# Expert results summed on chip: a gate-weighted one-hot product per pair of experts, in PSUM banks open for the layer

## The chip, the cores and the metric

One core of one Trainium2 chip runs the kernel. The metric is device time in microseconds of one execution. Engines: TensorE (PE; its weight loads are PEld), VectorE (DVE), ScalarE (ACT), GpSimd (POOL), SyncE (SP), and 16 DMA engines. PSUM has eight banks of 128 partitions x 512 fp32. All arithmetic is fp32.

## What is computed

One inference step of a two-layer encoder over 288 tokens (256 of a prompt, 32 of a sample), width 1024. Each layer has attention, an output projection, a layer norm, and then a mixture of 16 experts of which each token uses two. What the change touches is this last part:

```
gate = one_hot(the token's two experts) * their normalized scores      # (288, 16)
for e in range(16):
    h = silu(t @ w_gate[e]) * (t @ w_up[e])                            # 1024 -> 512
    y = y + gate[:, e:e + 1] * (h @ w_down[e])                         # 512 -> 1024
x = layernorm(ALPHA * x + y, ln2_g, ln2_b)
```

Between the layers, `x @ w_kv_shared` gives keys and values for layer 1; beside it stands a projection of the memory prompt with `w_mem_kv[1]`, which doesn't need x.

## The kernel before

Everything is written by hand: each engine has its own program, and semaphores order them. The tokens form three tiles (`TOKS`): 128, 128 and 32 rows, in `x_tok`.

**Routing.** VectorE works out for each token its two gates (`gates`) and two row numbers (`row_ab`): expert e has the rows 64e to 64e+63 (`CAP` = 64 slots). Tokens are sorted by expert through DRAM (`sorted_rows`), brought back, turned (`turn_rows`, L959) into `xs`, and each expert's 64 slots are copied to `xg`.

**One expert**, on TensorE, in the order that `expert_order` gives (up 0, up 1, down 0, turn, down 1, up 2, then for e from 3: up e, down e-1; at the end down 15):
- up(e), L916: 16 products, 64 slots stationary, 512 columns of gate and up weights moving, two halves of the array side by side, into bank e%2. ScalarE takes exp (L1378), VectorE forms the hidden values in four steps (L1832 to L1835).
- down(e): two transposes (L923) into bank 2, a copy by VectorE (`hidden_t`, L1825) for which TensorE waits some 0.5 us, then eight products (L930) into bank 3 or 4.
- ScalarE copies the result (L1400) and stores it with two transfers (L1403) to `expert_rows` in DRAM.

**Weights.** SP loads them, three experts ahead: gate and up of e+3 are asked for when up(e) has ended (L528), down of e+3 when down(e) has (L533).

**Combination.** After the stage GpSimd gathers each token's two rows (L2052), and VectorE multiplies them by the gates and adds them to ALPHA x (L1937, L1948). In layer 1 alone (`PAIR = (False, True)`) the last two experts aren't stored: ScalarE copies them into the two halves of `y_pair` (L1411), and TensorE adds them by a one-hot product (`add_tile`, L1026 and L1032) in PSUM, from which VectorE takes the statistics of the norm (L1927, L1932; L1736 finishes it).

**Between the layers** TensorE first turns the memory prompt (`memx1`, L1041) and projects it (`memkv1`, L1049), then turns x tile by tile (L679) and multiplies it by the shared weights (`kvs`, L1176). ScalarE empties memkv1's second bank (L1482, L1483) only after the root for tile 1's norm (L1365), and the same three banks serve kvs. SP asks for the first shared weights after tile 0's gathers.

**More than 64 tokens of one expert** are handled by branches (`more`) that this input doesn't take; both kernels have them.

Of the kernel before, what the change touches and what calls it, by code (L numbers as in the profile page):

```python
# [25 lines left out]
D = 1024  # L26
# [5 lines left out]
P = 128  # L32
# [17 lines left out]
PAIR = (False, True)  # L50
PAIR_ROW = ROWS - 2 * CAP
# [15 lines left out]
for _name, _n in (("ident", P), ("ones", P), ("tri", P), ("rotq", NT),  # L67
                  ("cost", 3 * 16), ("sint", 3 * 16), ("iota", 2 * CAP), ("rowbase", NE), ("tri4", EPG * EPG)):
    CONST[_name] = (_at, _n)
    _at += _n  # L70
CONST_W = _at

def shape_constants():
# [24 lines left out]
    put("rowbase", slice(None), np.arange(NE) * CAP)  # L98
    put("tri4", slice(None), np.tril(np.ones((EPG, EPG)), -1).reshape(-1))
# [7 lines left out]
def encoder_step(nc, ins, outs):  # L107
    ctx = ExitStack()
    with ctx:
# [50 lines left out]
        def cst(name, rows=slice(0, P)):  # L160
# [61 lines left out]
        y_pair = Region(gu_one_at + 6 * D).cut(2, 512)  # L222
# [6 lines left out]
        ln2_par = Region(xs_at).cut(2, D)  # L229

# [6 lines left out]
        act = zr.cut(2, 256)  # L237
        r_exp = zr.cut(48)
        score = zr.cut(48)
        biased = zr.cut(48)  # L240
        pair_hot = Region(zr.at).cut(3, 2 * CAP)
        gt = zr.cut(192)
        eq = zr.cut(192)
        pair_tmp = Region(zr.at).cut(2 * CAP)
# [14 lines left out]
        where = zr.cut(2, 48)  # L259
        col_ab = zr.cut(2, 3)  # L260
        row_ab = zr.cut(2, 3)
        fullest = zr.cut(1)
        y_at = zr.at
        y_out = zr.cut(2, 512)
        x_first = Region(y_at).cut(D)
        pair_t = zr.cut(NT)
        pair_row = zr.cut(2, 3)
        pair_keep = zr.cut(2, 3)
        pair_gate = zr.cut(2, 3)
# [7 lines left out]
        y_dram = nc.dram_tensor("expert_rows", (PASSES * ROWS, D), F32, kind="Internal").ap()  # L277
# [36 lines left out]
        ht_ready = sem("ht_ready"); ht_copied = sem("ht_copied"); down_done = sem("down_done"); y_copied = sem("y_copied")  # L314
        y_stored = [sem(f"y_stored{j}") for j in range(2)]
        back_in = [sem(f"back_in{t}") for t in range(3)]
        pair_ready = sem("pair_ready"); pair_turned = sem("pair_turned"); pair_taken = sem("pair_taken")
        pair_copied = sem("pair_copied"); part_ready = sem("part_ready"); tile_ready = sem("tile_ready")
        OV = ("ov_w", "ov_xg", "ov_gu", "ov_sig", "ov_h", "ov_ht", "ov_htc", "ov_y", "ov_yc", "ov_st", "ov_dve")
# [13 lines left out]
            ("memx1", "av" * 2), ("memkv1", "aa"), ("x2a", "av"), ("kvs0", "ava"), ("x2b", "av"), ("kvs1", "vav"), ("memt1", "av"), ("x2c", "a"),  # L333
# [76 lines left out]
        def stored(l):  # L410

            return NE // 2 - PAIR[l]

# [1682 lines left out]
```

## Time and profile before

| | us |
|---|---|
| median of three runs (917.15, 918.9, 918.55) | 918.55 |
| span of the profiled execution, first to last instruction | 916.5 |
| outside the span, against the median | 2.05 |
| PE / DVE / ACT / POOL busy in the span | 793.1 / 335.0 / 187.3 / 44.0 |
| expert stage of layer 0, from up(0) to the end of down(15) | 224.3 to 449.0 |
| expert stage of layer 1 | 674.7 to 896.1 |

The trace gives no time of its own for the profiled execution besides the span. A row of a timeline is a run of like instructions: start, length, engine, line, operation, output <- input, shape, how many, and in brackets how long the engine was idle before and what ended that. One fp32 product of up to 512 columns shows as two records of MATMUL; a transpose shows as one. A row that says "x32" at L916 is the 16 products of one expert.

### The profile page before, as it was taken

To read this page: it belongs to the slowest core of one execution; us is meant where nothing else is said; L and a number is where in the kernel's file an instruction comes from. 1 tells how busy PE (TensorE), PEld (TensorE's weight loads), DVE (VectorE), ACT (ScalarE), POOL (GpSimd) and SP (SyncE) were. 2 spreads that over 40 slices of the span, in tenths; PEclk is the share of its full clock that TensorE was granted. 3 is DMA by queue.
4 is the path that set the end of the run, shared out by engine and by line. 5 is a ranking of instruction groups with operands and counts; after the bars stand their busy time and mean duration, and the time that the engine had idled before them with its cause. 6 is when DMAs were issued, how large, how long until landed. Compare 5 with 4: busy or idle time off the path is not lost.

```text
span 916.5 us, 9955 instructions
## 1 busy us (share of the span) xinstructions
PE 793.1 (87%) x3943; PEld 387.2 (42%) x3943; DVE 335.0 (37%) x749; ACT 187.3 (20%) x452; POOL 44.0 (5%) x58
## 2 busy tenths in 40 slices
PE   6978999998899886876879989979898999777875
PEld 4665777453433222222334567654534333222221
DVE  1016455445422212122281054654533442122138
ACT  1213343110321101110110025620103211111101
POOL 1012000003000000000100000000020000000020
PEclk9998899899999999998989999999989999999998
DMA  9724007736999999999799060581679999999991
GB/s 357 232 72 196 1 1 297 300 153 239 402 424 423 425 428 422 425 426 424 265 350 361 3 261 1 215 330 53 275 282 424 431 423 429 422 428 423 428 398 57
DMA packets 43552, 272.80 MB, mean 298 GB/s; under 512 B 6360, under 2 KB 11166, under 8 KB 25840
## 3 DMA queue, kind: packets, MB, share of 16 engines
q1 hardware_dynamic: 32032, 243.69, 64.6%
q0 software_dynamic: 5888, 19.95, 6.5%
q10 hardware_dynamic: 5584, 8.51, 2.6%
q8 instruction: 32, 0.52, 0.2%
q14 instruction: 16, 0.13, 0.0%
HBM read 253.92 MB, written 18.21 MB: 297 GB/s over the span
## 4 chain that ended last, share of the span: by engine, by line
PE 56%; DMA 25%; DVE 9%; SPq 6%; ACT 2%; issue 1%; ACTq 0%; DVEq 0%
DMA arena<-in_expert_w_up 24%; PE bank L916 16%; PE bank L858 6%; PE bank L930 5%; PE bank L1176 5%; PE bank L845 3%; SPq L502 2%; PE bank L832 2%; PE bank L777 2%; PE bank L939 2%; PE bank L1049 2%; PE bank L825 1%; PE bank L679 1%; PE bank L1141 1%; PE bank L868 1%
## 5 line engine op out<-in xcount | busy, mean ns | idle before, releaser
L916 PE MATMUL bank<-arena 128*64 128x512 f32 x1024 | 240.7, 627 | 48.2 <-DMA arena<-in_expert_w_up 46.5
L916 PEld LDWEIGHTS bank<-arena 128*64 128x64 f32 x1024 | 77.2, 144 | 208.4 <-issue 148.8
L930 PE MATMUL bank<-arena 128*64 128x512 f32 x512 | 116.9, 598 | 16.7 <-DVE arena L1825 16.7
L1825 DVE COPY arena<-bank 128x256 f32<-128x256 f32 x32 | 13.6, 424 | 271.8 <-PE bank L923 271.8
L930 PEld LDWEIGHTS bank<-arena 128*64 128x64 f32 x512 | 34.1, 136 | 77.4 <-issue 54.6
L1378 ACT ACTIVATE arena<-bank 128x256 f32<-128x256 f32 x32 | 12.3, 384 | 265.8 <-PE bank L916 265.8
L1833 DVE RECIPROCAL arena<-arena 128x256 f32<-128x256 f32 x32 | 56.1, 1753 | 1.1
L858 PE MATMUL bank<-arena 128*128 128x512 f32 x128 | 56.0, 595 | 0.0
L1176 PE MATMUL bank<-arena 128*128 128x512 f32 x96 | 43.9, 619 | 6.6 <-ACT arena L1483 5.7
L1234 ACT COPY arena<-bank 128x512 f32<-128x512 f32 (+2 forms) x30 | 15.8, 537 | 112.9 <-PE bank L679 74.2
L858 PEld LDWEIGHTS bank<-arena 128*128 128x128 f32 x128 | 24.0, 190 | 29.6 <-issue 29.5
L1400 ACT COPY arena<-bank 128x512 f32<-128x512 f32 x30 | 17.6, 587 | 91.6 <-PE bank L930 91.6
L845 PE MATMUL bank<-arena 128*128 128x288 f32 x128 | 33.2, 412 | 0.0
L1382 ACT COPY arena<-arena 128x512 f32 x28 | 31.4, 1128 | 8.0 <-issue 7.2
L1176 PEld LDWEIGHTS bank<-arena 128*128 128x128 f32 x96 | 18.9, 199 | 30.3 <-issue 23.4
L1523 DVE COPY arena<-bank 128x512 f32<-128x512 f32 (+3 forms) x20 | 12.9, 649 | 49.5 <-PE bank L679 17.9
L679 PE MATMUL bank<-arena 128*128 128x128 f32 (+1 forms) x144 | 23.1, 320 | 8.0 <-DVE arena L1988 3.2
L1049 PE MATMUL bank<-arena 128*128 128x512 f32 x64 | 28.0, 595 | 1.0 <-DVE arena L1523 1.0
L2024 POOL DMA_DIRECT2D arena<-in_ln_g x4 | 2.3, 567 | 534.6 <-ACT arena L1382 313.5
L845 PEld LDWEIGHTS bank<-arena 128*128 128x128 f32 x128 | 23.7, 190 | 8.5 <-issue 2.7
L679 PEld LDWEIGHTS bank<-arena 128*128 128x128 f32 (+1 forms) x144 | 20.9, 202 | 13.8 <-issue 4.3
L777 PE MATMUL bank<-arena 128*128 128x64 f32 (+1 forms) x172 | 24.0, 280 | 1.3 <-DVE arena L1682 0.5
(272 smaller groups left out, 870.1 us busy)
## 6 DMA issues: line engine op xcount, KB each, us to landing
arena<-in_expert_w_gate SPq DMA_DIRECT2D x32, 2048.0 KB, 20.6
arena<-in_expert_w_up SPq DMA_DIRECT2D x32, 2048.0 KB, 25.6
arena<-in_expert_w_down SPq DMA_DIRECT2D x64, 1024.0 KB, 27.9
arena<-in_w_out SPq DMA_DIRECT2D x4, 2048.0 KB, 9.5
expert_rows<-arena ACTq DMA_DIRECT2D x60, 128.0 KB, 7.9
arena<-in_w_kv_shared SPq DMA_DIRECT2D x3, 2048.0 KB, 10.5
arena<-in_w_mem_kv SPq DMA_DIRECT2D x2, 2048.0 KB, 21.1
arena<-sorted_rows POOLq DMA_DIRECT2D x2, 2048.0 KB, 9.2
```

The costliest lines, as they stand in the source:

```text
L502: sp.dma_start(g_kv, ins["kv_norm_g"][0].partition_broadcast(P)).then_inc(small_in, 16)
L679: last = tr(b[:, k * n:(k + 1) * n], src[0:n, t, k0 + k::KC], ident[0:n, 0:n])
L777: last = mm(b[:, qt * w:(qt + 1) * w], pt[:, P * i:P * i + P], v[:, kt, h * w:(h + 1) * w], start=(i, kt) == mine_[0], stop=(i, kt) == min ...
L832: last = mm(b[:, 0:NT], w_q[:, k, 4 * g + hh, :], cq_feat[:, k, :], start=k == 0, stop=k == 2)
L845: last = mm(b[:, 0:NT], w_inb[k // 4][:, k % 4, P * c:P * c + P], x_feat[:, k, :], start=k == 0, stop=k == KC - 1)
L858: last = mm(b[:, :], x_feat[:, k, P * t:P * t + P], w_out[k // 4][:, k % 4, 512 * c:512 * (c + 1)], start=k == 0, stop=k == KC - 1)
L916: last = mm(bank[j][64 * half:64 * half + 64, :].rearrange("p (u f) -> p u f", u=2), slots[:, k, 0:CAP], w[:, :, k, 256 * half:256 * half ...
L930: last = mm(bank[3 + j][64 * n:64 * n + 64, :], hid_t[:, j, c, 64 * half:64 * half + 64], w[:, half, c, 512 * n:512 * n + 512], start=(hal ...
L1049: last = mm(b[:, :], feat[:, k, P * t:P * t + P], w[:, k, :], start=k == 0, stop=k == KC - 1)
L1176: last = mm(b[:, :], x_feat[:, k, P * t:P * (t + 1)], w_kvs[c][:, k, :], start=k == 0, stop=k == KC - 1)
L1382: return nc.scalar.copy(xg[:, j], xs[:, bass.ds(at, CAP), :].rearrange("p s k -> p k s"))
L1833: step(V.reciprocal(a, a))
```

## The change

The result of no expert goes to DRAM. For each pair p of experts (2p, 2p+1):
- ScalarE copies both results into the halves of `y_pair` (`keep`), for every expert.
- VectorE builds `hot[:, p%2, :]` (128 slots x 288 tokens): the gate where the slot's number is one of the token's two row numbers, else zero. For it the row numbers and gates were spread over all partitions once in the layer (`spread_rows`, 12 transposes behind `turn_rows`).
- TensorE multiplies: hot, for 128 tokens, stationary; `y_pair` moving (`add_pair`). The results of all eight pairs and ALPHA x (`add_x`, by the identity) add up in banks 5 and 6 (tile 0), 3 and 4 (tile 1) and 7 (sample, four strips of 32 partitions). ALPHA x is scaled at e = 4 instead of e = 14.

So that the banks stay free, the transposes of the hidden values go into the expert's own bank, down goes to bank 2 for every expert but the last (bank 0), and memx1 and memkv1 use banks 1 and 2. Gathers, stores and their waits are gone from the branch taken; the final norm of both layers reads PSUM, the sample tile after ScalarE has moved it to `x_tok`. The old pair code of layer 1 goes.

```diff
-PAIR = (False, True)
-PAIR_ROW = ROWS - 2 * CAP
+NP = NE // 2
...
-            ("memx1", "av" * 2), ("memkv1", "aa"), ...
+            ("memx1", "aaaa"), ("memkv1", "aa"), ...
...
         def sum_bank(t, c):
-            return bank[((0, 1), (5, 6), (2, 7))[t][c]]
+            return bank[((5, 6), (3, 4), (7, 7))[t][c]]
+        def down_bank(e):
+            return bank[0 if e == NE - 1 else 2]
...
             for e in range(3, NE):
+                if e % 2 and e >= 7:
+                    yield "sum", (e - 3) // 2
                 yield "up", e
+                if e % 2 and e < 7:
+                    yield "sum", (e - 3) // 2
                 yield "down", e - 1
             yield "down", NE - 1
...
-            sp.wait_ge(down_done, NE)
-            sp.wait_ge(back_in[0], 32)
+            sp.wait_ge(down_done, NE - 2)
             load_kvs(0)
...
+            def spread_rows(l):
+                pe.wait_ge(starts_ready, l + 1)
+                for i in (TURNS - 2, TURNS - 1):
+                    pe.wait_ge(*turn_taken(l, i))
+                for t, (a, n) in enumerate(TOKS):
+                    for q, v in enumerate((row_ab, gates)):
+                        for s in range(2):
+                            c = n * (2 * q + s)
+                            last = tr(bank[5 + t][:, c:c + n], v[0:n, s, t:t + 1].broadcast_to([n, P]), ident[0:n, 0:n])
+                    last.then_inc(spread_turned, 1)
+            def add_x(l, t):
+                a, n = TOKS[t]
+                pe.wait_ge(x_scaled, l + 1)
+                if t < 2:
+                    for c in range(2):
+                        mm(sum_bank(t, c)[:, :], ident, x_tok[:, t, 512 * c:512 * c + 512], start=False, stop=False)
+                else:
+                    for c in range(4):
+                        mm(sum_bank(2, 0)[DEC * c:DEC * (c + 1), 0:D // 4], ident[0:n, 0:n],
+                           x_tok[0:n, 2, D // 4 * c:D // 4 * (c + 1)], start=False, stop=False, tile_position=(0, DEC * c))
+            def add_pair(l, p):
+                pe.wait_ge(hot_ready, NP * l + p + 1)
+                pe.wait_ge(kept, 2 * (NE * l + 2 * p + 2))
+                for t in (0, 2, 1):
+                    a, n = TOKS[t]
+                    v = hot[:, p % 2, a:a + n]
+                    if t < 2:
+                        for c in range(2):
+                            last = mm(sum_bank(t, c)[:, :], v, y_pair[:, c, :], start=p == 0, stop=p == NP - 1)
+                    else:
+                        for c in range(4):
+                            last = mm(sum_bank(2, 0)[DEC * c:DEC * (c + 1), 0:D // 4], v,
+                                      y_pair[:, c // 2, D // 4 * (c % 2):D // 4 * (c % 2 + 1)],
+                                      start=p == 0, stop=p == NP - 1, tile_position=(0, DEC * c))
+                    if p == NP - 1:
+                        last.then_inc(tile_ready, 1)
+                if p < NP - 1:
+                    last.then_inc(summed, 1)
...
-                    if e > 1:
-                        pe.wait_ge(y_copied, copied(l, e - 2))
+                    if 0 < NE * l + e and e < NE - 1:
+                        pe.wait_ge(kept, 2 * (NE * l + e))
+                    expert_down(down_bank(e), e % 2, dn[e % 3]).then_inc(down_done, 1)
...
+                        add_pair(l, e)
+                        if 2 <= e < 5:
+                            add_x(l, e - 2)
...
+                add_pair(l, NP - 1)
...
-                def store(e):
-                    nc.scalar.copy(y_out[:, j, :], bank[3 + j][:, :]).then_inc(y_copied, 1)
-                    for n in range(2):
-                        ac.dma_start(y_dram[CAP * e:CAP * (e + 1), 512 * n:512 * n + 512],
-                                     y_out[64 * n:64 * n + 64, j, :]).then_inc(y_stored[j], 16)
                 def keep(e):
+                    j = e % 2
+                    ac.wait_ge(down_done, NE * l + e + 1)
                     for n in range(2):
                         nc.scalar.copy(y_pair[64 * j:64 * j + 64, n, :],
+                                       down_bank(e)[64 * n:64 * n + 64, :]).then_inc(kept, 1)
...
-                if l == 0:
-                    copies("memx1", mem_dst(mem_feat1))
+                ac.wait_ge(tile_ready, 3 * l + 2)
+                for c in range(4):
+                    own(nc.scalar.copy(x_tok[0:DEC, 2, D // 4 * c:D // 4 * (c + 1)],
+                                       sum_bank(2, 0)[DEC * c:DEC * (c + 1), 0:D // 4]), sample_moved if c == 3 else None)
                 for t in range(3):
                     root(2 * l + 1, t)
+                    if l == 0 and t == 0:
+                        copies("memx1", mem_dst(mem_feat1))
...
+                def hots(p):
+                    if NP * l + p >= 2:
+                        ve.wait_ge(summed, max((NP - 1) * l + p - 1, (NP - 1) * l))
+                    if l and p < 2:
+                        ve.wait_ge(tile_ready, 3 * l)
+                    h, at = hot[:, p % 2, :], cst("slot")[:, p:p + 1]
+                    own(stt(h, spread[:, 0, :], at, spread[:, 2, :], ALU.is_equal, ALU.mult))
+                    step(stt(hot_b, spread[:, 1, :], at, spread[:, 3, :], ALU.is_equal, ALU.mult))
+                    own(tt(h, h, hot_b, ALU.add), hot_ready)
...
                 for e in range(3, NE):
                     turned(e - 1)
                     form(e)
+                    if e % 2:
+                        hots(e // 2)
-                    if e == NE - 2:
+                    if e == 4:
                         for t in range(3):
                             own(ts(x_tok[:, t, :], x_tok[:, t, :], ALPHA, None, ALU.mult), x_scaled if t == 2 else None)
```

## Rows read from the trace of the kernel before

**Rows 1.** The page: its first line.
```profile
span 916.5 us, 9955 instructions
```

**Rows 2.** Timeline of PE, expert stage of layer 0 and behind it.
```profile
242.78 2.06 PE L959 MATMUL bank<-arena 128*128 128x128 f32 x16
...
295.04 7.04 PE L916 MATMUL bank<-arena 128*64 128x512 f32 x32
...
306.51 7.04 PE L916 MATMUL bank<-arena 128*64 128x512 f32 x32
...
320.10 7.09 PE L916 MATMUL bank<-arena 128*64 128x512 f32 x32 [1.94 <-DMA arena<-in_expert_w_up]
...
335.47 8.78 PE L916 MATMUL bank<-arena 128*64 128x512 f32 x32 [3.68 <-DMA arena<-in_expert_w_up]
...
430.70 9.16 PE L916 MATMUL bank<-arena 128*64 128x512 f32 x32 [6.14 <-DMA arena<-in_expert_w_up]
439.79 0.51 PE L923 MATMUL bank<-arena 128*128 128x128 f32 x2
...
449.01 1.59 PE L1041 MATMUL bank<-arena 128*128 128x128 f32 x12
...
454.23 13.97 PE L1049 MATMUL bank<-arena 128*128 128x512 f32 x32 [0.99 <-DVE arena L1523]
...
474.80 5.48 PE L1176 MATMUL bank<-arena 128*128 128x512 f32 x7 [5.72 <-ACT arena L1483]
```

**Rows 3.** The page's DMA issues: KB each, median us to landing.
```profile
arena<-in_expert_w_gate SPq DMA_DIRECT2D x32, 2048.0 KB, 20.6
...
arena<-in_expert_w_down SPq DMA_DIRECT2D x64, 1024.0 KB, 27.9
...
expert_rows<-arena ACTq DMA_DIRECT2D x60, 128.0 KB, 7.9
```

**Rows 4.** Windows of the stages: PE, PEld, DVE, ACT, POOL busy, clock, DMA share, GB/s.
```profile
249.20:318.10 68.90, 65.79 (x301) 22.04 (x300) 19.86 (x31) 14.79 (x20) 0.52 (x1) 1.00 1.01 425
318.10:449.10 131.00, 100.75 (x421) 31.95 (x420) 27.99 (x44) 15.14 (x23) 1.09 (x2) 0.93 1.00 419
...
780.60:896.10 115.50, 90.47 (x370) 28.25 (x368) 27.42 (x42) 13.61 (x21) 6.70 (x8) 0.93 0.99 412
```

**Rows 5.** Timeline of PE, expert stage of layer 1 and its end.
```profile
768.96 7.04 PE L916 MATMUL bank<-arena 128*64 128x512 f32 x32
...
783.19 8.70 PE L916 MATMUL bank<-arena 128*64 128x512 f32 x32 [2.58 <-DMA arena<-in_expert_w_up]
...
896.11 1.98 PE L1026 MATMUL bank<-arena 128*128 128x512 f32 x4
...
899.65 1.88 PE L1026 MATMUL bank<-arena 128*128 128x512 f32 x4
901.37 1.88 PE L1032 MATMUL bank<-arena 128*128 128x512 f32 x4
903.17 1.90 PE L1026 MATMUL bank<-arena 32*32 32x512 f32 x4
```

**Rows 6.** Chain that ended last, in order of time: start, us, engine, line.
```profile
474.80 23.08 PE bank L1176 x48
...
499.60 20.84 PE bank L1176 x48
...
610.85 3.66 PE bank L868 x64
```

**Rows 7.** Timeline of all engines behind layer 1's expert stage.
```profile
893.37 7.86 DVE L1948 SCALAR_TENSOR_TENSOR arena<-arena 128x1024 f32<-128x1024 f32 x6 [0.89 <-issue]
...
896.23 1.18 ACT L1411 COPY arena<-bank 64x512 f32<-64x512 f32 x2 [3.42 <-PE bank L930]
...
901.26 1.30 DVE L1927 BATCH_NORM_STATS2 arena<-bank 128x6 f32<-128x512 f32 x2
...
914.20 0.33 SPq L625 DMA_DIRECT2D out_y_sample<-arena  x1
```

More of the change, by code:

```diff
@@ L405, in loads @@
             return l * len(range(e % 3, NE, 3)) + e // 3 + 1
-        def stores(l, e):
-            return sum(stored(m) for m in range(l)) + e // 2 + 1
-        def stored(l):
-            return NE // 2 - PAIR[l]
-        def copied(l, e):
-            return sum(2 * stored(m) for m in range(l)) + e + 1
-        def pairs(l):
-            return sum(PAIR[:l])
         def sum_bank(t, c):
-            return bank[((0, 1), (5, 6), (2, 7))[t][c]]
+            return bank[((5, 6), (3, 4), (7, 7))[t][c]]
+        def down_bank(e):
+            return bank[0 if e == NE - 1 else 2]
         def expert_order():
@@ L1204, in _ @@
             experts(1)
-            for t in range(3):
-                add_tile(1, t)
         @block.scalar
@@ L1419, in experts @@
                 gate(1)
-                store(0)
+                keep(0)
                 for i in range(0, TURNS, 2):
@@ L1429, in experts @@
                 take(3)
-                store(1)
+                keep(1)
                 gate(2)
@@ L1436, in experts @@
                         take(e + 2)
-                    (keep if PAIR[l] and e == NE - 1 else store)(e - 1)
-                (keep if PAIR[l] else store)(NE - 1)
+                    keep(e - 1)
+                keep(NE - 1)
                 ac.wait_ge(starts_ready, l + 1)
@@ L1442, in experts @@
                     o = ov[l]
-                    for j in range(2):
-                        ac.wait_ge(y_stored[j], 32 * stores(l, 2 * stored(l) - 1))
                     with ac.Fori(0, NE) as e:
@@ L1865, in experts @@
                 form(2)
+                for t, (a, n) in enumerate(TOKS):
+                    ve.wait_ge(spread_turned, 3 * l + t + 1)
+                    own(V.tensor_copy(spread[:, :, a:a + n], bank[5 + t][:, 0:4 * n].rearrange("p (q n) -> p q n", n=n)))
+                own.settle()
+                hots(0)
                 for e in range(3, NE):
@@ new lines, in combine @@
+                    for c in range(2):
+                        own(V.bn_stats(bn[0:n, t, 6 * c:6 * c + 6], sums[c]))
+                    own.settle()
+                    step(V.bn_aggr(mean_var[0:n, t, :], bn[0:n, t, :]), var_ready)
+                    ve.wait_ge(ln_in, 32 * (2 * l + 2))
+                    for c in range(2):
+                        own(stt(x_tok[0:n, t, 512 * c:512 * c + 512], sums[c], mean_var[0:n, t, 0:1],
+                                ln2_par[0:n, 0, 512 * c:512 * c + 512], ALU.subtract, ALU.mult))
@@ L2057, in layer @@
                     ln_load(ln2_par, "ln2_g", "ln2_b", l)
-                    for j in range(2):
-                        po.wait_ge(y_stored[j], 32 * stores(l, 2 * stored(l) - 1))
-                    bring_back(PAIR_ROW if PAIR[l] else ROWS)
                 with po.If(more > 0):
```

171 lines of the change are left out of this document (57 added, 114 removed).

## The prediction

> **What bounds the kernel now.** I read the page first (span and busy engines), then the PE timeline of both expert stages, then the windows, the DMA issues, and last the stretch behind each stage. The page gives a span of 916.5 us; the runs' median is 918.55 us, so 2.05 us lie outside the span, and I make the sum on the span [rows 1]. In the PE timeline one expert takes 11.47 us when nothing blocks it: up(6) starts at 295.04, up(7) at 306.51 [rows 2]. From up(8) on, each up waits for its weights (1.94 us, 3.68 us, at the end 6.14 us). An expert's weights are one gate, one up and two down transfers, 6.29 MB [rows 3], and the DMA engines are full at 419 GB/s over the stretch and 425 GB/s in the stretch before, which I use [rows 4]: 14.8 us, and 15.4 us with the 0.26 MB that the expert's result takes on its way to DRAM. So the late stage is bound by DMA, the early one by TensorE, and what matters is how much TensorE time the late waits can swallow.
>
> **That slack, worked out.** Layer 0: without waits up(15) would start at 306.51 + 8 x 11.47 = 398.3. Its 16 products take 6.97 us, and from its end (439.79) to the end of down(15) (449.01) are 9.22 us, so the stage would end at 414.5 instead of 449.0: slack 34.5 us. This includes the slower products after a wait (8.78 instead of 7.04 us) [rows 2]. Layer 1: 768.96 + 7 x 11.47 + 6.97 + 9.22 = 865.4 against 896.1: slack 30.7 us [rows 5].
>
> **What is added on TensorE, for each layer.**
> - A pair's sum: for the two prompt tiles four products of 128x128 by 512 columns. The same shape ran in the old last-pair sum: four took 896.11 to 899.65, 3.54 us [rows 5]. The sample tile is four products side by side, 32 wide, 256 columns; the output projection does eight such sets in 3.66 us, 0.46 us a set [rows 6]. A change of the array's tiling costs 1.80 against 1.72 us, 0.08 us [rows 5]; with two or three more of them a pair costs 4.2 us. Seven sums lie before the last down: 29.4 us.
> - The Trainium skill (TensorEngine Tiling (Array Packing), Key Properties) says that a change of tiling mode drains TensorE, which speaks against a sum wedged between two 64-wide stages. It prices nothing; the row beside it shows 0.08 us.
> - Adding scaled x: four such prompt products, 3.5 us, and a sample set 0.5: 4.0 us.
> - Spreading rows and gates: 12 transposes. 16 took 2.06 us [rows 2], so 1.4 us, and 0.7 us until the last banks of the turn are emptied. ScalarE comes 0.6 us earlier to the turn (it issues no stores). Net 1.5 us.
> - A new wait. From e=7 on, the sum stands directly behind down(e-2), whose result it needs. ScalarE must copy both halves first: in the old last pair it began 0.1 us after the products and took 1.18 us [rows 7]. TensorE stands still about 1.4 us, and behind it in the queue are up(e) and all that follows. Five sums (2 to 6) have it: 7.0 us. Sums 0 and 1 follow an up, and their copies are long done.
> - The sum is 29.4 + 4.0 + 1.5 + 7.0 = 41.9 us; in layer 1 the old pair's three transposes go, 0.6 us, so 41.3.
>
> VectorE's one-hots (three operations on 288 columns for a pair, some 1.4 us, between the 0.42 and 0.69 us rows of 256 and 512 columns) cost nothing: they run under the next up, which takes 7 us. Without that cover they would delay the hidden_t copy by as much. Bounds for the unknown: the sum of a pair is at least 3.9 (no tiling cost) and at most 4.8 us; the copy wait between 0 and 2 us.
>
> **What is removed.** 0.26 MB of stores an expert, 0.62 us of DMA each at 425 GB/s. With 14 of them ahead of up(15), the weights of up(15) could land 8.6 us sooner, at 422.1. But TensorE now comes to up(15) at 398.3 + 41.9 = 440.2, so the weights have been there for 18 us. At up(8) the gap is about the same (TensorE at 335, weights at 316). A pair takes TensorE 22.9 + 4.2 + 1.4 = 28.5 us and DMA 29.6 us: both keep nearly the same pace, TensorE never catches up its lag, and the freed DMA time buys nothing. The stores on ScalarE's queue go too; nothing waited for them.
>
> So the end of down(15) moves by 41.9 - 34.5 = +7.4 us in layer 0, and by 41.3 - 30.7 = +10.6 us in layer 1.
>
> **Behind the stages.** Layer 0: stores, gathers and combination lay beside the memory projection already. What was left is the start of the shared K/V product at 474.80, 25.8 us after down(15), 5.7 of them a wait on tile 1's statistics, through ScalarE's copy [rows 2]; and that product then ran 23.08 instead of 20.84 us [rows 6]. Now the queue is: copy wait 1.4, last sum 4.2, the mem transposes (2.1 us, and 1.0 us of waits on ScalarE, which first moves the sample tile, loads its table and takes tile 0's root, and now empties all four banks), 13.9 of projection, 1.1 and 0.7 for tile 0: about 25.0. With the faster product that makes -3.0 us. The K/V weights are asked for at once after down(15) and are needed 25 us later. Layer 1: VectorE had 7.86 us of combining, and only from 901.26 the last three norms, 12.9 us, to 914.20 [rows 7]. Now the first statistics start 1.4 + 1.8 + 0.1 = 3.3 us behind down(15) instead of 5.2; the root waits 0.5 longer for ScalarE. That is -1.4 us.
>
> **Sum:** 916.5 + 7.4 - 3.0 + 10.6 - 1.4 = 930.1 us of span, 932 us of time: slower.
>
> **The rivals.**
> - *DMA sets the end.* If the additions ahead of up(15) fit under the waits, the stage ends with its last weights: 8.6 us earlier in each layer. It decides from additions below 34.5 - 8.6 = 26 us (layer 1: 22); I have 42. Total 918.6 - 17.2 - 4.4 = 897 us. For it: the DMA share of 1.00 in this stretch [rows 4]; against it: the shapes of the products are measured in this trace. The Trainium skill (Perfetto Trace Analysis, Roofline) gives 16 DMA engines about 435 GB/s as a single core's ceiling; read by that rule alone the kernel sits at its roof and each byte less is time, which is this rival with its 897 us.
> - *The copy waits cost nothing.* If the waits of sums 2 to 6 lie under something that I don't see, 14 us go: 918 us, no change.
> - *The clock falls.* After waits of 1.94 us the next up took 7.09 us [rows 2], after 2.58 us it took 8.70 [rows 5]. The granted clock is 0.93 in the late stretch [rows 4]. If the 1.4 us wait, with the 0.5 us ones beside it, brings this on, ten ups lose 1.7 us each: 949 us.
> - *The change doesn't do what it says*: the sum of the last pair existed before, so this is no open question.
>
> **How the numbers follow.** Forecast (924 to 941 us) 0.68, DMA sets the end 0.11, no copy waits 0.12, clock 0.09. The low bounds of the costs (3.9 and 0 us) reach to 917, the high ones (4.8 us, 2 us) to 943 and beyond; the range 917 to 942 leaves out the DMA case and the clock. Within 0.2% (some 1.8 us, about what can be told from no change) fall about two thirds of the no-wait case and a little of the forecast: same 0.09; faster 0.13, slower 0.78.
>
> **What the changed profile would show.** PE without DMA waits in the expert stages, clock 1.00 there, up(e) at 6.97 us throughout; seven sums of 4.2 us in each stage; PE idle of 1.4 us ahead of sums 2 to 6, released by ScalarE's half copies; DMA share below 1.00 late in the stage; first K/V product without the 5.7 us wait. If up(15) still waits for weights, the DMA rival holds, and the prediction is wrong in its size and perhaps its sign.

## The result: 3.5% slower, and the profile after

The changed kernel took 950.24 us (median of four: 943.41, 946.36, 954.12, 954.34) against 918.59 us for the kernel before: ratio 1.0347 [1.0287, 1.0408]. Forecast were 932 us, 917 to 942. The sign was right and the size was not; the time lies outside the range. The profiled execution is the 954.12 us one. Ratios leave out executions more than 1.5% above the fastest of the same kernel (two of the four of stores_back below, the profiled one among them), so a ratio need not be that of the two medians given. The page of the changed kernel, lines of its head and its groups:

```profile
span 952.3 us, 10508 instructions
...
PE 860.6 (90%) x4228; PEld 416.8 (44%) x4228; DVE 340.0 (36%) x781; ACT 208.4 (22%) x492; POOL 32.6 (3%) x46
...
L908 PE MATMUL bank<-arena 128*64 128x512 f32 x1024 | 225.1, 593 | 1.8 <-DVE arena L1813 1.8
...
L987 PE MATMUL bank<-arena 128*128 128x512 f32 x128 | 63.1, 616 | 16.5 <-ACT arena L1419 16.5
...
arena<-in_expert_w_up SPq DMA_DIRECT2D x32, 2048.0 KB, 15.8
```

Two readings. L908 is the up product (L916 before): its group now has 1.8 us of idle time ahead of it in the whole span, and none for weights. L987 is the new sum over a pair: 63.1 us busy, and 16.5 us of idle time ended by ScalarE's copy of an expert's result (L1419). Its 16.5 us are twelve waits of 1.37. Up weights land 15.8 us after they are asked for; in the kernel before it was 25.6. The TensorE timeline of the changed kernel, layer 0's stage and behind it:

```profile
252.35 1.40 PE L963 MATMUL bank<-arena 128*128 128x128 f32 x12 [0.80 <-DVE arena L1870]
253.68 0.50 PE L915 MATMUL bank<-arena 128*128 128x128 f32 x2
254.70 5.35 PE L922 MATMUL bank<-arena 128*64 128x512 f32 x16 [0.52 <-DVE arena L1838]
...
300.85 1.98 PE L987 MATMUL bank<-arena 128*128 128x512 f32 x4
302.76 0.64 PE L990 MATMUL bank<-arena 128*32 128x256 f32 x8
303.33 1.98 PE L987 MATMUL bank<-arena 128*128 128x512 f32 x4
305.15 0.39 PE L915 MATMUL bank<-arena 128*128 128x128 f32 x2
...
413.29 1.95 PE L987 MATMUL bank<-arena 128*128 128x512 f32 x4 [1.37 <-ACT arena L1419]
...
417.66 7.09 PE L908 MATMUL bank<-arena 128*64 128x512 f32 x32
...
442.19 1.96 PE L987 MATMUL bank<-arena 128*128 128x512 f32 x4 [1.37 <-ACT arena L1419]
...
492.34 22.56 PE L1198 MATMUL bank<-arena 128*128 128x512 f32 x48 [3.09 <-ACT arena L1493]
```

- A sum behind an up takes 305.15 - 300.85 = 4.30 us (forecast 4.2).
- A sum behind a down stands still for 1.37 us first, as forecast. From one such sum to the next are 442.19 - 413.29 = 28.90 us, 5.96 more than two experts alone (2 x 11.47, [rows 2]).
- Down(1) (254.70) takes 5.35 us, the same products elsewhere 3.65. This wasn't forecast.
- The shared K/V product (L1198) still waits, for the same copy as before; forecast was that this wait would go. It runs 22.56 us, not 20.84.

The windows of the changed kernel (columns as in [rows 4]): ahead of layer 0's stage, its second half, and the stretch ahead of layer 1's stage.

```profile
0.00:227.20 227.20, 205.68 (x1139) 135.58 (x1140) 87.03 (x253) 56.89 (x162) 19.47 (x28) 0.92 0.48 183
...
320.90:462.80 141.90, 129.86 (x566) 43.22 (x564) 35.91 (x61) 22.95 (x36) 1.09 (x2) 1.00 0.87 361
...
627.80:695.90 68.10, 63.45 (x254) 31.95 (x254) 27.98 (x72) 5.82 (x13) 6.97 (x8) 0.86 0.48 194
```

And the first and last of these stretches in the kernel before:

```profile
0.00:224.30 224.30, 200.55 (x1139) 132.69 (x1139) 86.93 (x253) 56.86 (x162) 20.07 (x28) 0.95 0.49 187
...
610.90:674.70 63.80, 59.16 (x254) 29.80 (x255) 28.00 (x72) 5.83 (x13) 7.01 (x8) 0.92 0.51 205
```

Late in the stage the clock is now 1.00 and the DMA share 0.87 (before 0.93 and 1.00, [rows 4]): TensorE sets the pace. But 2.9 and 4.3 us more also stand in stretches with the same instruction counts in which nothing was edited, and there the granted clock differs: 0.92 against 0.95, 0.86 against 0.92. To see how much of the gap is such a difference between executions, the changed kernel was run again beside the experiments.

Landmarks of all runs (us). The stage runs from up(0) to the end of down(15); "to K/V" from there to the first shared K/V product.

| | before | after | again | three | three_mid | before_mid |
|---|---|---|---|---|---|---|
| up(0), layer 0 | 224.3 | 227.2 | 222.5 | 227.8 | 220.8 | 219.6 |
| stage, layer 0 | 224.7 | 235.6 | 236.9 | 224.6 | 218.8 | 223.5 |
| to K/V | 25.8 | 29.6 | 27.9 | 25.6 | 25.6 | 28.6 |
| stage, layer 1 | 221.5 | 236.9 | 236.9 | 224.6 | 218.8 | 221.3 |
| span | 916.5 | 952.3 | 943.0 | 919.7 | 902.8 | 918.5 |

### The profile page after: what moved, and what is told of

Its sections match the earlier page's. It is cut to its first block, busy times and chain, and to the rows that moved or that the text cites. A ratio compares the mean times of both kernels' runs of the same rounds, so it can differ in the third digit from the quotient of the medians.

```text
span 952.3 us, 10508 instructions
## 1 busy us (share of the span) xinstructions
PE 860.6 (90%) x4228; PEld 416.8 (44%) x4228; DVE 340.0 (36%) x781; ACT 208.4 (22%) x492; POOL 32.6 (3%) x46
## 4 chain that ended last, share of the span: by engine, by line
PE 79%; DVE 9%; SPq 6%; ACT 4%; issue 2%; DMA 0%; ACTq 0%; DVEq 0%
PE bank L908 23%; PE bank L922 12%; PE bank L987 6%; PE bank L850 6%; PE bank L1198 5%; PE bank L837 3%; SPq L495 2%; PE bank L824 2%; PE bank L769 2%; PE bank L931 2%; ACT arena L1419 2%; PE bank L1069 2%; PE bank L671 1%; DVE arena L1838 1%; PE bank L817 1%
## 5 line engine op out<-in xcount | busy, mean ns | idle before, releaser
L908 PE MATMUL bank<-arena 128*64 128x512 f32 x1024 | 225.1, 593 | 1.8 <-DVE arena L1813 1.8
L908 PEld LDWEIGHTS bank<-arena 128*64 128x64 f32 x1024 | 74.2, 137 | 146.8 <-issue 146.8
L922 PE MATMUL bank<-arena 128*64 128x512 f32 x512 | 121.4, 618 | 16.5 <-DVE arena L1838 16.5
L1838 DVE COPY arena<-bank 128x256 f32<-128x256 f32 x32 | 13.6, 424 | 274.2 <-PE bank L915 274.2
L987 PE MATMUL bank<-arena 128*128 128x512 f32 x128 | 63.1, 616 | 16.5 <-ACT arena L1419 16.5
L922 PEld LDWEIGHTS bank<-arena 128*64 128x64 f32 x512 | 34.9, 141 | 81.0 <-issue 58.1
L1398 ACT ACTIVATE arena<-bank 128x256 f32<-128x256 f32 x32 | 12.3, 383 | 254.2 <-PE bank L908 254.2
L1419 ACT COPY arena<-bank 64x512 f32<-64x512 f32 x64 | 37.1, 580 | 123.2 <-PE bank L922 122.5
L850 PE MATMUL bank<-arena 128*128 128x512 f32 x128 | 56.0, 596 | 0.0
L1198 PE MATMUL bank<-arena 128*128 128x512 f32 x96 | 43.4, 614 | 3.9 <-ACT arena L1493 3.1
L987 PEld LDWEIGHTS bank<-arena 128*128 128x128 f32 x128 | 21.7, 189 | 51.8 <-issue 50.2
L850 PEld LDWEIGHTS bank<-arena 128*128 128x128 f32 x128 | 24.0, 190 | 29.6 <-issue 29.5
L1069 PE MATMUL bank<-arena 128*128 128x512 f32 x64 | 31.2, 650 | 1.9 <-DMA arena<-in_w_mem_kv 1.0
L1198 PEld LDWEIGHTS bank<-arena 128*128 128x128 f32 x96 | 18.6, 196 | 27.4 <-issue 23.1
L837 PEld LDWEIGHTS bank<-arena 128*128 128x128 f32 x128 | 23.7, 190 | 8.5 <-issue 2.7
## 6 DMA issues: line engine op xcount, KB each, us to landing
arena<-in_expert_w_up SPq DMA_DIRECT2D x32, 2048.0 KB, 15.8
```

Of the source, the lines that this page charges most:

```text
L837: last = mm(b[:, 0:NT], w_inb[k // 4][:, k % 4, P * c:P * c + P], x_feat[:, k, :], start=k == 0, stop=k == KC - 1)
L850: last = mm(b[:, :], x_feat[:, k, P * t:P * t + P], w_out[k // 4][:, k % 4, 512 * c:512 * (c + 1)], start=k == 0, stop=k == KC - 1)
L908: last = mm(bank[j][64 * half:64 * half + 64, :].rearrange("p (u f) -> p u f", u=2), slots[:, k, 0:CAP], w[:, :, k, 256 * half:256 * half ...
L922: last = mm(b[64 * n:64 * n + 64, :], hid_t[:, j, c, 64 * half:64 * half + 64], w[:, half, c, 512 * n:512 * n + 512], start=(half, c) == ( ...
L987: last = mm(sum_bank(t, c)[:, :], v, y_pair[:, c, :], start=p == 0, stop=p == NP - 1)
L1069: last = mm(b[:, :], feat[:, k, P * t:P * t + P], w[:, k, :], start=k == 0, stop=k == KC - 1)
```

## The experiments

Theory: TensorE sets the pace of the changed stages; what was added to its queue, the copy waits among it, is the loss. Rivals: DMA still sets the end; the copy waits lie under something else. Each diff is against the changed kernel unless it says otherwise.

### again: the changed kernel, unchanged

> The changed kernel once more, nothing altered, for a second profile. Its four times lie 11 us apart, those of the kernel before 2 us, and in the first profile stretches whose code is the same in both kernels are 7 us longer (2.9 ahead of layer 0's expert stage, 4.3 ahead of layer 1's) at a lower granted clock (0.92 for 0.95, 0.86 for 0.92). Theory A (the clock falls by chance of when a wait comes, and costs what lies above the stages' own 24 us): again 941 to 955 us, and in the new profile these two stretches come out at other lengths, while both expert stages stay within 2 us of 235.6 and 236.9. Theory B (something of the change makes these stretches longer each time): the same 7 us in the same two places.

944.36 us (941.31 to 953.96, six runs), before 918.58 (914.6 to 928.64): ratio 1.0299 [1.0237, 1.0361]. Its span is 943.0 us. Its timeline, TensorE, the turn with the spread, down(1), and the K/V product:

```profile
245.79 1.10 PE L951 MATMUL bank<-arena 64*128 64x64 f32 x8 [0.22 <-ACT arena L1431]
247.69 1.53 PE L963 MATMUL bank<-arena 128*128 128x128 f32 x12 [0.80 <-DVE arena L1870]
249.15 0.70 PE L915 MATMUL bank<-arena 128*128 128x128 f32 x2
250.37 6.25 PE L922 MATMUL bank<-arena 128*64 128x512 f32 x16 [0.52 <-DVE arena L1838]
...
487.21 13.12 PE L1198 MATMUL bank<-arena 128*128 128x512 f32 x26 [3.09 <-ACT arena L1493]
```

The stages (236.9 us each), the slow down(1) and the K/V wait recur; the two long stretches of the first profile don't (222.5 and 63.9 us here). The two profiles are 9.3 us apart though the kernel is the same, and this one is the one that I take the terms from. Its windows over down(1) and the start of the next up:

```profile
250.40:253.50 3.10, 3.10 (x8) 0.97 (x10) 0.00 (x0) 0.30 (x1) 0.00 (x0) 0.50 0.97 415
253.50:256.60 3.10, 3.10 (x12) 0.95 (x10) 0.00 (x0) 0.00 (x0) 0.00 (x0) 0.65 0.99 420
256.60:260.00 3.40, 3.40 (x20) 1.09 (x16) 0.00 (x0) 1.16 (x2) 0.00 (x0) 1.00 1.01 398
```

The slow down(1) is the clock: it starts at 0.50 (1.2 GHz) and is back at 1.00 (2.4 GHz) in the up behind it. The clock was falling already in the spread transposes; first again's window over them, then the window over the whole turn in the kernel before:

```profile
247.50:250.30 2.80, 2.16 (x14) 1.57 (x14) 0.45 (x2) 1.78 (x3) 0.00 (x0) 0.73 1.01 433
...
242.80:250.20 7.40, 5.69 (x44) 5.05 (x42) 4.98 (x6) 5.31 (x6) 0.52 (x1) 1.00 1.02 433
```

The kernel before has waits of 1.03 and 0.23 us between its turn's transposes, and its clock stays at 1.00 there and in down(1) (3.65 us). What releases the K/V product is seen in ScalarE's timeline of the same execution:

```profile
483.72 0.58 ACT L1254 COPY arena<-bank 128x512 f32<-128x512 f32 x1 [6.66 <-PE bank L671]
...
486.33 0.29 ACT L1385 ACTIVATE arena<-arena 128x1 f32<-128x1 f32 x1 [2.03 <-DVE arena L1946]
486.53 0.35 ACT L1492 COPY arena<-bank 128x256 f32<-128x256 f32 x1
486.79 0.38 ACT L1493 COPY arena<-bank 128x256 f32<-128x256 f32 x1
```

TensorE's wait is for x2a's copy, which is done at 484.3. But ScalarE's copies are counted in job order, and memkv1's second pair of copies (L1492, L1493) comes ahead of x2a in that order and is made only behind tile 1's root (L1385). So the count is short by them until 487.17. The bank can't be the reason: memkv1's second bank is now one of banks 1 and 2, the K/V product's are 5 to 7, and the wait is still there.

### sum_after_up: every sum behind an up

```diff
-                if e % 2 and e >= 7:
-                    yield "sum", (e - 3) // 2
                 yield "up", e
-                if e % 2 and e < 7:
+                if e % 2:
                     yield "sum", (e - 3) // 2
```

> Sums 2 to 6 stand behind the next up, as sums 0 and 1 do, so that the copies of the pair's second result are done when TensorE comes to the sum. Main theory (TensorE sets the pace of both stages, so that each of its waits counts): the 1.37 us wait goes from five sums in each layer, stage 0 about 228.7 and stage 1 about 230 us, together -14 us: 936 of a median of 950. Rival (the waits lie where TensorE would have waited for weights anyway): within 3 us of the changed kernel.

929.68 us (926.81 to 936.58), ratio 1.0112 [1.0045, 1.018]. TensorE's timeline of this kernel, one pair:

```profile
323.75 7.04 PE L906 MATMUL bank<-arena 128*64 128x512 f32 x32
330.71 1.98 PE L985 MATMUL bank<-arena 128*128 128x512 f32 x4
...
337.64 3.65 PE L920 MATMUL bank<-arena 128*64 128x512 f32 x16 [0.52 <-DVE arena L1836]
```

No wait stands ahead of the sum: a pair is 27.14 us long instead of 28.91. Stages 227.4 and 226.6 us, 9.4 and 10.3 shorter than in again. Five waits with what goes with them make 8.9 of it, 1.77 us each by the pair's length; the rest is down(1), which in this profile took 4.92 and 5.00 us instead of again's 6.25 and 6.42, less a 0.85 us wait for the sorted rows in layer 0. That refutes the rival "the copy waits cost nothing".

### stores_back: the results stored again, besides the sums

```diff
+                    if 7 * l + e // 2 > 0:
+                        ac.wait_ge(y_stored[j], 32 * (7 * l + e // 2))
                     for n in range(2):
                         nc.scalar.copy(y_pair[64 * j:64 * j + 64, n, :], ...
...
+                    if e < NE - 2:
+                        ac.wait_ge(kept, 2 * (NE * l + e) + 2)
+                        for n in range(2):
+                            ac.dma_start(y_dram[CAP * e:CAP * (e + 1), 512 * n:512 * n + 512],
+                                         y_pair[64 * j:64 * j + 64, n, :]).then_inc(y_stored[j], 16)
```

> The changed kernel, and ScalarE also stores the results of experts 0 to 13 to DRAM as before (two transfers of 128 KB each from y_pair; nothing reads them). Main theory (the DMA time that the missing stores freed buys nothing, because TensorE comes 18 us after the weights): within 3 us of the changed kernel, 950, and no wait of TensorE for weights. Rival (the stage is bound by DMA still): 0.62 us for each of 28 experts, 17 us more: 967.

947.89 us (932.79 to 958.44), ratio 1.0194 [1.0113, 1.0275], an interval that overlaps again's. The profile is of the longest execution (958.44 us); what is read from it are the stages. Both took 238.0 us, 1.2 more than in again, with no wait for weights. The window over the stretch that stands above for the changed kernel:

```profile
320.90:462.80 141.90, 129.86 (x566) 43.28 (x567) 38.50 (x65) 23.66 (x37) 1.09 (x2) 1.00 0.93 393
```

TensorE is as busy as in the changed kernel (129.86 us, clock 1.00) while the DMA engines move 393 GB/s instead of 361. Had DMA set the end, 0.26 MB an expert would have brought the late stage back to waits for weights as in [rows 2]. The 1.2 us are no DMA time either: in the turn of the rows TensorE waits 1.64 us for ScalarE instead of 0.42, and just ahead of that copy ScalarE spends 1.18 us on issuing expert 0's two stores. The DMA traffic that the change removes was worth about nothing to it.

### no_prompt_sums: the prompt products of sums 1 to 6 and of ALPHA x left out

```diff
-                for t in (0, 2, 1):
+                for t in (0, 2, 1) if p in (0, NP - 1) else (2,):
...
-                        if 2 <= e < 5:
+                        if e == 4:
                             add_x(l, e - 2)
```

> Left out: the products of the two prompt tiles in sums 1 to 6, and ALPHA x of the prompt tiles; the waits, copies, one-hots and the sample tile's products stay. This takes about 26 us a layer off TensorE, which leaves some 19 us of additions, below the 26 us from which DMA should set the end. Main theory (two regimes: the later of TensorE and DMA): the waits for weights come back, and the stages end with the last weights, 8.6 us sooner than in the kernel before: stage 0 about 217 us, stage 1 about 214 us, the whole near 908 us. Rival (TensorE's added products aren't what costs): less than 20 us below the changed kernel's 950.

2780.43 us, but that time says nothing: layer 1 now computes with another x, which sends over 64 tokens to one expert, and the branches for that ran. Only layer 0's stage is read, 218.1 us. TensorE's timeline there:

```profile
405.10 7.09 PE L908 MATMUL bank<-arena 128*64 128x512 f32 x32 [1.49 <-DMA arena<-in_expert_w_up]
...
422.33 9.02 PE L908 MATMUL bank<-arena 128*64 128x512 f32 x32 [3.52 <-DMA arena<-in_expert_w_up]
```

With most of the sums' work gone, the waits for weights come back and the stage stops there, 6.6 us shorter than before the change. That is about where the weights alone would end a stage without stores; the rival named 8.6 us. The changed stage, at 236.9 us, ends 18.8 us later.

### memkv_first: memkv1's second bank emptied ahead of x2a's copies

```diff
                     if l == 0 and t == 1:
+                        k, b = next(memkv1)
+                        own(nc.scalar.copy(mem_raw1[:, 0, k, :], b[:, 0:MW]))
+                        out_of(nc.scalar.copy(mem_v1[:, k, :], b[:, MW:2 * MW]))
                         copies("x2a", feat_dst)
                     root(2 * l + 1, t)
...
-                    if l == 0 and t < 2:
+                    if l == 0 and t < 1:
                         k, b = next(memkv1)
```

> ScalarE empties the second bank of the memory projection before it copies tile 0's features and takes tile 1's root, as the order of jobs counts it. In the changed kernel the first shared K/V product still waits 3.09 us for that copy, though the two no longer share a bank. Theory (the wait is for a count in the order of jobs, not for the bank: TensorE asks for tile 0's features by how many copies ScalarE has ended, and the memory copy is one of them): the wait goes, -3 us, and -1.7 us more where the product then runs at the full clock: 940 to 942 of 944 to 950. Rival (tile 1's statistics are needed by the product in some other way): no change, and the wait stays with another releaser.

945.95 us (936.47 to 946.6), ratio 1.0246 [1.0188, 1.0305]. The whole time can't be told from again's; the stretch can. TensorE's timeline:

```profile
491.62 13.54 PE L1198 MATMUL bank<-arena 128*128 128x512 f32 x31 [0.83 <-ACT arena L1254]
```

The wait went from 3.09 to 0.83 us and is now for x2a's own copy. The product begins 25.6 us behind down(15) instead of 27.9, and from its start to layer 1's attention are 51.1 us instead of 52.9. So 4.0 us come back, and the stretch is 2.5 us shorter than before the change (to its start -0.2, from there 51.1 against 53.4), near the forecast's -3.0. Of the 4.0 us, 2.3 are the wait. The other 1.7 are the clock at the product's start, and they don't hang on the wait alone, as the next run's profile shows.

### spread_later: the 12 spread transposes behind up(2) instead of behind the turn

```diff
                         turn_rows(l)
-                        spread_rows(l)
...
+                    if (what, e) == ("up", 2):
+                        spread_rows(l)
```

> The 12 transposes that spread row numbers and gates stand behind up(2) instead of between the turn of the rows and down(1). In all profiles of the changed kernel down(1) takes 5.35 to 6.42 us, in the kernel before 3.65 us in both layers. Theory (the waits of 0.41, 0.23 and 0.80 us with the transposes between them pull the clock down, and the spread's own wait is the last of them): down(1) back at 3.65 us, no 0.80 us wait, -3.4 us in each layer, together -7. Rival (down(1) is slow because of something at its banks): the spread moves and down(1) stays slow; at most -1.6 us for the two waits.

941.19 us (938.34 to 950.08), ratio 1.0259 [1.0202, 1.0315]. Both stages 233.2 us, 3.6 shorter than in again. TensorE's timeline:

```profile
253.77 3.65 PE L922 MATMUL bank<-arena 128*64 128x512 f32 x16 [0.53 <-DVE arena L1839]
...
264.22 1.43 PE L963 MATMUL bank<-arena 128*128 128x128 f32 x12
```

The transposes cost the same 1.4 us. What went is the 0.80 us wait ahead of them and, in both layers, the slow down(1): 3.65 us instead of 6.25 and 6.42. Over all profiles, down(1) took 4.92 to 6.42 us in the eleven stages with the spread ahead of it (no_prompt_sums' second not counted), and 3.65 us in every stage without. The window over down(1) in this kernel:

```profile
253.80:257.40 3.60, 3.60 (x18) 1.31 (x20) 0.00 (x0) 2.15 (x2) 0.00 (x0) 1.00 0.98 419
```

Its clock is 1.00, where again had 0.50 and then 0.65. The edit moves the transposes and the wait together, so which of the two brings the clock down isn't separated. The K/V product of this kernel:

```profile
489.53 20.87 PE L1199 MATMUL bank<-arena 128*128 128x512 f32 x48 [3.09 <-ACT arena L1494]
```

It waits 3.09 us and yet runs at full speed. In the other five profiles with that wait it started at a lower clock and took some 22.5 us; in all five with 0.83 us it took 20.84.

### three: sum_after_up, memkv_first and spread_later together

The three diffs above, and nothing else.

> The three edits together: sums behind the up, memory copy first, spread behind up(2). If they are independent: 929.7 (the sums alone) - 5 - 7 = 918 us, level with the kernel before; expert stages 224 us each (before 224.7 and 221.5). If the clock gives back less: 922 us.

920.75 us (915.38 to 923.47, twelve runs), ratio 0.9991 [0.9963, 1.002]: no difference from before. Stages 224.6 us each, 12.3 shorter than in again (the two edits alone: 9.4 or 10.3, and 3.6, but the first of these had part of down(1)'s loss in it): five waits 8.9, the spread's wait 0.8, down(1) 2.6. Order alone takes the loss away, though the products of the sums remain in TensorE's queue.

### three_mid: three, and the hidden values turned in the middle of the next up

```diff
-            def expert_up(j, w, slots):
+            def expert_up(j, w, slots, middle=None):
                 for k in range(KC):
+                    if k == KC // 2 and middle:
+                        middle()
...
-                    expert_up(e % 2, ups[e % 3], xg[:, e % 2]).then_inc(up_done, 1)
+                    expert_up(e % 2, ups[e % 3], xg[:, e % 2],
+                              (lambda: turn(e - 1)) if e in (1, *range(3, NE)) else None).then_inc(up_done, 1)
+                def turn(e):
+                    pe.wait_ge(h_ready, NE * l + e + 1)
+                    expert_turn(e % 2).then_inc(ht_ready, 1)
                 def down(e):
...
-                    pe.wait_ge(h_ready, at)
-                    expert_turn(e % 2).then_inc(ht_ready, 1)
+                    if e in (1, NE - 1):
+                        turn(e)
                     pe.wait_ge(ht_copied, at)
```

> The same, and the two transposes of the hidden values of e-1 stand in the middle of up(e) from e=3 on, so that VectorE's copy (0.52 us of waiting before each down) lies under the other half of the up. A pair then costs TensorE 22.9 + 4.2 - 1.0 = 26.1 us, well below the 29.6 us of its weights. Main theory (the later of the two sets the end): the stages come to 219 to 221 us, close to the 216 us that the weights allow in layer 0 (213 in layer 1), with waits for weights back at the last experts; total 908 to 913 us, faster than the kernel before. Rival (transposes inside an up cost more than they hide, by changes of the array's tiling): 918 or more.

904.5 us (902.63 to 908.87, six runs), ratio 0.9833 [0.9796, 0.987]: faster than both kernels. TensorE's timeline of layer 1:

```profile
852.17 3.60 PE L908 MATMUL bank<-arena 128*64 128x512 f32 x16
855.71 0.50 PE L915 MATMUL bank<-arena 128*128 128x128 f32 x2
856.14 3.65 PE L908 MATMUL bank<-arena 128*64 128x512 f32 x16
859.62 3.60 PE L922 MATMUL bank<-arena 128*64 128x512 f32 x16
```

The 0.5 us wait for VectorE's copy ahead of down is gone from the middle of the stage, since half an up covers it. Its windows:

```profile
780.00:870.00 90.00, 90.00 (x402) 30.23 (x400) 26.17 (x43) 16.39 (x26) 1.09 (x2) 1.00 0.98 416
```

TensorE is busy in all of the 90 us at clock 1.00, and the DMA share is 0.98: both limits are nearly met. Stages 218.8 us each.

### before_mid: the same turning in the kernel before

> The kernel before with only this edit: the two transposes of the hidden values of e-1 in the middle of up(e). The same edit took 5.8 us from each expert stage where TensorE sets the pace. Main theory (in the kernel before the late stage waits for weights, so TensorE time saved there is waited away): at most 1 us a layer, 916 to 919 of 918.6 to 920.3. Rival (a cheaper TensorE stage is worth as much here): 5.8 us a layer, 908.

918.87 us (913.3 to 927.38, twelve runs), ratio 0.999 [0.9946, 1.0033]. Stages 223.5 and 221.3 us. The same edit that takes 5.8 us from each stage of three takes 1.2 and 0.2 from those of the kernel before. TensorE's timeline of layer 1:

```profile
846.99 5.11 PE L918 MATMUL bank<-arena 128*64 128x512 f32 x16 [2.60 <-DMA arena<-in_expert_w_up]
...
880.54 5.35 PE L918 MATMUL bank<-arena 128*64 128x512 f32 x16 [4.91 <-DMA arena<-in_expert_w_up]
```

And the windows of the stretch that stands above:

```profile
780.00:870.00 90.00, 73.47 (x290) 22.89 (x288) 19.88 (x30) 12.21 (x17) 1.09 (x2) 0.89 1.01 425
```

In the kernel before, the same 90 us show 70.53 us of PE and a clock of 0.92. The waits for up weights add up to 50.6 us in the two stages, in the kernel before to 46.4. Time saved on TensorE turns into longer waits for weights and slower products behind them where DMA sets the pace, and into a shorter stage where it doesn't. This is the plainest evidence that the change moved the stages from the one limit to the other.

### light1, light1_stores: three_mid with layer 1's sums lightened, without and with its stores

light1 leaves out the prompt products of sums 1 to 6 in layer 1, so its output is not the full sum; light1_stores also stores experts 0 to 13 of layer 1, as in stores_back.

```diff
-                for t in (0, 2, 1):
+                for t in (0, 2, 1) if l == 0 or p in (0, NP - 1) else (2,):
```

> The version with the transposes in the middle of the ups, and left out in layer 1: the prompt tiles' products of sums 1 to 6 (22 us of TensorE). Layer 1's stage is 218.8 us with them, without one wait for weights. Main theory (the later of TensorE and DMA): TensorE alone would need 197 us, so the weights set the end, 8 us earlier than in the kernel before by the missing stores: 213 us, with waits for weights at the late ups. Rival (no floor by DMA at this place, the stage follows TensorE down): 197 us.

> The same, and in layer 1 ScalarE stores the results of experts 0 to 13 to DRAM again. This is the price of the stores where DMA does set the end. Main theory: 0.62 us for each store pair ahead of the last weights, 13 of them, 8 us more than light1: stage 1 at 221 us. Rival (stores and loads don't share what is short): stage 1 as in light1.

light1: 905.32 us (899.44 to 911.87), ratio 0.9806 [0.9733, 0.9879]. light1_stores: 907.2 (904.73 to 919.94), ratio 0.9894 [0.9816, 0.9973]. Stage of layer 1: 219.5 and 224.3 us. TensorE's timeline, up(15), in light1:

```profile
872.34 5.35 PE L908 MATMUL bank<-arena 128*64 128x512 f32 x16 [4.11 <-DMA arena<-in_expert_w_up]
```

and in light1_stores:

```profile
864.11 6.36 PE L909 MATMUL bank<-arena 128*64 128x512 f32 x16 [6.97 <-DMA arena<-in_expert_w_up]
```

Once TensorE is quick enough, weights set the pace again and stores have a price: 4.8 us for 14 experts, where 0.62 us each would make 8.6. Both stages missed the expectation (213 and 221 us). One reason is seen: up(0) came 8.9 and 9.9 us behind the sorted rows' pack, not 13.25 as before, so the start of the stage moved against its DMA work. Counted from the pack, up(15) starts at 210.2 us in light1, 215.0 in light1_stores and 216.8 in the kernel before (878.18 - 661.41). The two stages don't begin alike either. Their first 9 us, light1 and then light1_stores:

```profile
671.00:680.00 9.00, 9.00 (x42) 3.63 (x44) 5.17 (x22) 0.38 (x1) 1.83 (x3) 1.00 0.52 157
...
659.00:668.00 9.00, 9.00 (x42) 3.63 (x44) 5.14 (x22) 0.38 (x1) 1.34 (x2) 1.00 0.69 241
```

The second moved 0.76 MB more in them, 1.8 us of DMA time at 425 GB/s by my estimate. So 4.8 us is probably a low reading, from one profile of each; the rest of the 3.8 us isn't explained, and the whole times (905.32 and 907.2) don't tell the two apart.

## Why the prediction was right on what sets the pace and wrong in its size

Taken on again's profile (span 943.0, gap 26.5 us):

| step | forecast | measured |
|---|---|---|
| ahead of layer 0's stage | 0 | -1.8 |
| stage, layer 0 | +7.4 | +12.1 |
| between the stages | -3.0 | +1.5 |
| stage, layer 1 | +10.6 | +15.4 |
| behind it | -1.4 | -0.8 |
| sum | +13.6 | +26.4 |

**The slack and who sets the pace: right.** No wait for weights is left, up takes 6.97 to 7.09 us, the clock is 1.00 but around down(1). The stage without additions ends at 190.2 us by the prediction's sum, so the additions measure 236.85 - 190.2 = 46.7 us, not 41.9.

**The pair's sum and the copy wait: right in kind, small by 2.0 us.** Sums 0 and 1: 2 x 4.3. Sums 2 to 6: 5 x 5.96 = 29.8, forecast 5 x 5.6. The wait was 1.37 us as forecast (1.4), the sum 4.3 to 4.4; 0.2 us a pair I can't place. The changes of tiling fit: by the old rows two prompt parts at 3.44 and a sample set at 0.46 make 3.9 us, so 4.30 leaves 0.4 for three of them (from up's tiling, to the sample's and back; the transposes behind keep the prompt's), 0.1 to 0.2 us each by this estimate. On the drain of which the Trainium skill speaks (TensorEngine Tiling (Array Packing), Key Properties): the trace agrees that it costs something, by the estimate above 0.1 to 0.2 us a change.

**Adding ALPHA x: right**, 4.2 us against 4.0.

**The spread: the step that failed in the stages.** Its transposes and the wait cost 2.1 us less the 0.6 that ScalarE comes sooner, the forecast's 1.5. I looked no further than the transposes. But behind them down(1) took 6.25 us in layer 0 and 6.42 in layer 1 instead of 3.65: +2.6 and +2.8 us. spread_later shows it, since the same transposes behind a full up leave down(1) at 3.65; whether the 12 transposes or the 0.80 us wait bring the clock down stays open. The forecast had named such a fall of the clock, but placed it behind the copy waits, where the up took 7.09 us: it did not happen there.

The terms in layer 0 then are 8.6 + 29.8 + 4.2 + 1.5 + 2.6 = 46.7 us.

**Between the stages: failed.** I put the 5.7 us wait of the K/V product down to tile 1's statistics, through ScalarE's copy out of a bank that the product shares; the change separates the banks, so I left the wait out. It is a wait on a count in job order, and the count stayed behind a copy that ScalarE makes late. So 3.09 us stayed, and the product ran 22.56 us instead of 20.84. memkv_first moves that one copy and gives -2.5 us where -3.0 was forecast: the arithmetic held, the reason for the wait did not. That the product runs at full speed without the long wait is borne out in five profiles, but spread_later had 20.87 us with the wait, so 1.7 us of this term vary with the execution. Together the spread and this stretch are 2.6 + 2.8 + 4.5 = 9.9 of the 12.8 us missed in the span; the pairs' sums, 2.0 us a layer, are 4.0 more, and the stretches ahead and behind, unedited or nearly so, take 1.2 back.

**The range** was cut too narrow at its low end: 3.9 us in 14 sums and no wait at ten make 932 - 4.2 - 14 = 914 us, not 917. It didn't matter here. Its high end, 942, lies 2.4 us below the later median, 944.36.

**The rivals.** *DMA sets the end* is refuted by stores_back; no_prompt_sums and light1 show what it needs: more than half of the additions gone. On the ceiling that the Trainium skill names (Perfetto Trace Analysis, Roofline): late in the changed stage the DMA engines move 361 GB/s, and fewer bytes bought nothing there; the trace agrees where weights set the pace, as in before_mid, with 425 GB/s. *The copy waits cost nothing* is refuted by sum_after_up. *The clock falls* was named with its 949 us. That the first median, 950.24, lies beside it is luck: the clock fell at down(1) and not at ten ups, and some 6 us of that median were gone when the same kernel was run again.

**What stays open.** The first profile is 9.3 us longer than again's. The timeline and windows place 4.7 us ahead of layer 0's stage and 4.3 us in the stretch from outs1 to the pack (54.8 us; again 50.6), both with a lower granted clock; the memory projection behind layer 0's stage is 1.7 us longer too, and that stage 1.2 us shorter. The chain of the first profile shows it in one row, the output projection, 3.66 us before [rows 6]:

```profile
627.80 6.52 PE bank L860 x64
```

before_mid shows the same 54.8 us in a kernel without the change, so the change isn't needed for it; what decides it isn't settled. The changed kernel's runs lie over 13 us and those of before over 14, and the median moved with that: 950.24 in one set of runs, 944.36 in the next.

## What to carry to other kernels

When work moves from a bound queue (DMA) to another engine, work out first how much time that engine has to give in the stage; here it was 31 to 35 us a layer, and 46 to 47 were put in. Where it stands in the queue is then worth as much as what it is: the same products behind an up and away from short waits cost 12 us less a stage, and with one copy moved the change was even with the kernel before. A wait on a counter is a wait for everything counted before it, so look at the order of the count before ascribing a wait to a bank or a buffer.

## What the runs showed of the hardware

- Short transposes with waits of 0.42, 0.22 and 0.80 us between them, and 0.52 us ahead of down(1), were followed by eight fp32 products (16 records) that began at a granted clock of 0.50 (again): 4.92 to 6.42 us in eleven stages instead of 3.65. Without the 0.80 us wait and the 12 transposes they ran at 1.00 (spread_later; also in the kernel before, where the turn has waits of 1.03 and 0.23 us). The copy wait of 1.37 us between long products was followed by ups of 7.09 us at most.
- The same wait of 3.09 us behind eight transposes was followed by a slower start of the K/V product in five profiles (22.5 to 22.6 us) and not in a sixth (20.87 us, spread_later).
- The same code ahead of the first stage took 218.8 to 229.4 us over the thirteen profiles, and its granted clock 0.92 or 0.95 in the two shown above.
- A change of TensorE's tiling between fp32 products costs 0.1 to 0.2 us, an estimate from 4.30 us for a sum of 3.9 us of products.
- Issuing two stores took ScalarE 1.18 us, and where TensorE waited for ScalarE's next copy that was the stores' whole price to the stage (1.2 us, stores_back).
